# A state-space scan with its u and gate products in three passes on split operands, x split once for the scan and the heads

## The chip, the cores and the metric

The kernel is one program on one core of a Trainium2 chip. The metric is the device time of one execution in microseconds. TensorE is called PE in the rows, its weight loads PEld, VectorE DVE, ScalarE ACT, GpSimd POOL and the queue that issues the DMAs SP.

## What is computed

The program runs two transformer blocks one after the other, in fp32. The change lies in the mixer of the second block, which works on 512 tokens of width 1024. Of the reference it is this:

```
u = rmsnorm(x, mix_norm)
proj = u @ w_in
u_ssm, q, k, v, xq, g_ssm, g_attn, g_mem = jnp.split(proj, cuts, axis=-1)
y_ssm = jax.nn.gelu(s5_scan(u_ssm, ssm_a_re, ssm_a_im, ssm_log_dt, ssm_b_re, ssm_b_im,
                            ssm_c_re, ssm_c_im, ssm_d))
...
merged = (jax.nn.sigmoid(g_ssm) * br_ssm + jax.nn.sigmoid(g_attn) * br_attn
          + jax.nn.sigmoid(g_mem) * br_mem)
```

`s5_scan` is, for each of 32 groups of 16 channels, the recurrence x_t = A x_{t-1} + B u_t over 64 complex states, and y_t = Re(C x_t) + D u_t.

## The kernel before

Activations lie transposed, channels on the 128 partitions and the 512 tokens along the row, so x is 8 slices of 128 x 512 (KC is 8). A weight chunk is 128 x 1024: eight blocks of 128 x 128, which one product turns into one 128 x 512 output in PSUM. The accumulator `acc` is all of PSUM, eight banks of 128 x 512.

The mixer (`mixer_stage`) runs three stages one after the other, each a block with its own program for every engine: `scan_stage`, `heads_stage` and `out_stage`. Within a stage an engine runs its instructions in the order of the code, and semaphores are the only tie between engines; they start at 1. There is no scheduler.

**The scan stage** normalises x to `xn` (`m_xn`; L2082 on VectorE), and makes from it four chunks of u (L1944) and 24 chunks of gates (L1953), all with fp32 matmuls; one such matmul of 128 x 512 shows as two records in the trace. The four u chunks come as one load `s_w`; the gate chunks come through a ring of three buffers, `s_gw`. Then come small matrices: `b_wide` and `c_wide` are made by VectorE, transposed on TensorE (L1963, L1973) and copied by ScalarE to `s_b_t` and `s_c_t`.

The scan itself is a loop over SC = 16 steps of 128 complex states each:

- GpSimd makes the step's turns, the rotation by the angle at every token, with six operations of 128 x 512 (L1925 to L1928), in three buffers; it waits until step s-3 has used its buffer.
- TensorE makes the step's inputs (L1983, two fp32 matmuls, four records) two steps ahead.
- VectorE turns, scans and turns back (L2104 to L2126) and releases `scanned` with the last operation.
- TensorE then adds C times the state to y (L1998, four records).

The 24 gate products are spread over the steps: `at_step[s]` has two in an even step and one in an odd one. TensorE's order in step s is: the gates of s, the wait for `scanned` of s, y of s, inputs of s+2. ScalarE takes each gate from its bank through a sigmoid (L2018) and SP stores it.

**The heads stage** needs the same normed x for the query, key and value products. It does them in three passes on split operands: an operand is rounded to a shorter format on ScalarE (`hi`, type fp32r), the rest is what a subtraction of the rounded from the full value leaves (`lo`), and the product is hi x hi + hi x lo + lo x hi, three matmuls in place of one fp32 matmul. There x is rounded by ScalarE (L2517, L2520) and its rest taken by VectorE (L2648), and of each weight chunk ScalarE rounds (L2451) and GpSimd takes the rest (L2269), in a ring of four. Later the heads keep their queries and keys in the room of `xn`.

Of the kernel before, what the change touches and what calls it, by code (L numbers as in the profile page):

```python
# [69 lines left out]
        "c_in u_there gw0 gw1 gw2 sq_a sq_d summed rooted normed u_mm u_ready b_wid c_wid b_turned c_turned "  # L70
        "b_taken c_taken shape spun rotated bu_mm scanned y_mm y_pre gate_mm gated steady"),
    "d_": (
        "c_bd c_mem w0 w1 w2 w3 rounded split x_hi x_lo m_hi m_lo m_sq m_part m_mm m_root m_on proj_mm ev_a "
        "ev_d v_turn v_there scored logits expd weighed turned pt_there pv_mm took x_scored x_max x_exp "
        "x_weighed x_turned x_pt x_pv x_took"),
# [17 lines left out]
def build(nc, x_t, meta_t, mem_t, bias_onehot, dil_onehot, rel_bias, dil_table, gains, wi, wo, w_out,  # L93
# [3 lines left out]
    with top:  # L97
# [1590 lines left out]
        def mixer_stage(tables):  # L1688
            with ExitStack() as st:
# [3 lines left out]
                with ExitStack() as s1:  # L1693
                    xn = sb(s1, "m_xn", [P, KC, SEQ])
                    with ExitStack() as s2:
                        scan_stage(s2, xn, yg, tables)
                    with ExitStack() as s2:
                        heads_stage(s2, xn, at_, xa)
# [144 lines left out]
        def scan_stage(st, xn, yg, tables):  # L1843
# [7 lines left out]
            EARLY = 0  # L1851
            u = sb(st, "s_u_t", [P, 4, SEQ])
            b_t = sb(st, "s_b_t", [P, 2, 4, P])
            c_t = sb(st, "s_c_t", [P, 2, SC, P])
            d = sb(st, "s_dt", [P, 4])
            gw = sb(st, "s_gw", [P, 3, KC * P])
            gates = sb(st, "s_gates", [P, GATES_HELD, SEQ])
            w = sb(st, "s_w", [P, 4, KC * P])
# [11 lines left out]
            spare = sb(st, "s_spare", [P, SEQ])  # L1870
            rstd = spare
# [4 lines left out]
            (c_in, u_there, gw0, gw1, gw2, sq_a, sq_d, summed, rooted, normed, u_mm, u_ready, b_wid, c_wid, b_turned,  # L1876
             c_turned, b_taken, c_taken, shape, spun, rotated, bu_mm, scanned, y_mm, y_pre,
             gate_mm, gated, steady) = sems(st, "s_")
            gate_there = [gw0, gw1, gw2]
            at_step = [[n for n in range(EARLY, GATES) if (n - EARLY) * SC // (GATES - EARLY) == s] for s in range(SC)]  # L1880

            with nc.Block() as block:
                @block.sync
                def _(sp):
                    def store_gate(sp, n):
# [3 lines left out]
                    sp.dma_start(w[:, :, :], s_u.rearrange("c p n -> p c n")).then_inc(u_there, 16)  # L1889
# [4 lines left out]
                    for n in range(GATES):  # L1894
                        if n >= 3:
                            sp.wait_ge(gate_mm, 1 + n - 2)
                        sp.dma_start(gw[:, n % 3, :], gate_w[n]).then_inc(gate_there[n % 3], 16)
                        if n >= 3:
                            store_gate(sp, n - 3)
                    for n in range(GATES - 3, GATES):  # L1900
                        store_gate(sp, n)

                @block.gpsimd
                def _(pool):
# [6 lines left out]
                                       pattern=[[16, 8]], channel_multiplier=-1).then_inc(shape, 1)  # L1911
                    t = t_spare[:, :].rearrange("p (a b) -> p a b", a=COARSE)
                    for s in range(SC):
# [18 lines left out]
                        pool.drain()  # L1932
                    arm(pool, "d_")

                @block.tensor
                def _(pe):
                    pe.wait_ge(sq_a, 2)
                    pe.matmul(acc[:, 6, :], ones[:, :], nsq[:, 0, :], start=False, stop=True).then_inc(summed, 1)
                    pe.wait_ge(u_there, 17)
# [17 lines left out]
                    for n in range(EARLY):  # L1957
                        gate(n)
# [1106 lines left out]
```

## Time and profile before

| | us |
|---|---|
| median of three runs | 3737.55 (3736.84 to 3737.74) |
| the profiled execution | 3736.37 |
| its span, first to last instruction | 3734.7 |
| mean granted clock of TensorE | 0.976 |
| scan stage up to its first gate product, from 2691.5 | 48.4 |
| scan loop, 2739.90 to 2961.93 | 222.0 |
| end of the loop to the first matmul of the heads, 2972.55 | 10.6 |

In a timeline each row is one instruction, or several alike in a row (xN): start, length from the start of the first to the end of the last, engine, line, tiles written and read, and in brackets the idle time of that engine ahead of it with what ended it. Lengths of matmuls that follow each other overlap, so the time of one is read from start to start. In a windows row PEclk is TensorE's granted clock, in parts of 2.4 GHz.

### The profile page before, as it was taken

The numbers are of one execution on the slowest core, as the hardware profiler recorded it, in microseconds if no ns is written. First come the engines' busy times: TensorE is split into PE (matmuls) and PEld (weight loads), VectorE is DVE, ScalarE is ACT, GpSimd is POOL, SyncE is SP. The second block draws the span as 40 slices with busy tenths as digits, with TensorE's granted clock in tenths as the row PEclk, the third lists the DMA queues.
The fourth block names the chain that finished last, engine by engine and source line by source line (L and its number), as shares of the span: only waits on it lengthen the run. The fifth ranks groups of instructions, "written<-read, shape, count | busy, mean of one in ns | idle before, by whom it ended". The sixth has DMA issues, their size and how long they took to land. (4 is left out here: it accounts for less than half of the span.)

```text
span 3734.7 us, 50566 instructions
## 1 busy us (share of the span) xinstructions
PE 3566.8 (96%) x20104; PEld 2920.9 (78%) x20104; DVE 1741.1 (47%) x2492; ACT 1300.1 (35%) x1793; POOL 440.0 (12%) x465
## 2 busy tenths in 40 slices
PE   8999799799999999989999999999999899799998
PEld 7999777699999999755547888888744477678886
DVE  5442466544434443266625443443377533545433
ACT  4332266433323332134525432342110243324421
POOL 0000222100000000010006400000144233220000
PEclk9999899899999999989999999999999999999999
DMA  4322311022222222300013222222212421233222
GB/s 168 135 88 85 122 55 51 18 91 90 83 85 102 90 86 78 136 26 23 1 34 113 101 88 103 101 90 90 101 51 85 120 78 51 107 108 108 94 85 84
DMA packets 116172, 318.07 MB, mean 85 GB/s; under 512 B 13815, under 2 KB 56951, under 8 KB 100052
## 3 DMA queue, kind: packets, MB, share of 16 engines
q1 hardware_dynamic: 116052, 316.51, 25.0%
q8 instruction: 70, 1.15, 0.1%
q14 instruction: 50, 0.41, 0.0%
HBM read 307.98 MB, written 17.01 MB: 87 GB/s over the span
## 5 line engine op out<-in xcount | busy, mean ns | idle before, releaser
L332 PE MATMUL acc<-fb_xh,fb_wh 128*128 128x264 f32 x1408 | 287.8, 286 | 5.5 <-DVE fb_wl L489 5.5
L332 PE MATMUL acc<-fb_xl,fb_wh 128*128 128x264 f32 x1408 | 288.1, 286 | 0.0
L332 PE MATMUL acc<-fb_xh,fb_wl 128*128 128x264 f32 x1408 | 287.7, 286 | 0.0
L332 PE MATMUL acc<-fd_xh,fd_wh 128*128 128x512 f32 x704 | 275.6, 391 | 5.5 <-DVE fd_wl L489 5.5
L332 PE MATMUL acc<-fd_xl,fd_wh 128*128 128x512 f32 x704 | 274.6, 390 | 0.0
L332 PE MATMUL acc<-fd_xh,fd_wl 128*128 128x512 f32 x704 | 274.6, 390 | 0.0
L332 PEld LDWEIGHTS acc<-fb_xh,fb_wh 128*128 128x128 f32 x1408 | 220.1, 189 | 5.8 <-DVE fb_wl L489 5.7
L407 ACT ACTIVATE fb_wh<-fb_raw 128x2048 fp32r<-128x2048 f32 (+1 forms) x74 | 124.7, 1686 | 286.9 <-PE acc L391 173.8
L332 PEld LDWEIGHTS acc<-fb_xl,fb_wh 128*128 128x128 f32 x1408 | 219.3, 189 | 0.0
L332 PEld LDWEIGHTS acc<-fb_xh,fb_wl 128*128 128x128 f32 x1408 | 219.0, 189 | 0.0
L484 DVE TENSOR_TENSOR fb_wl<-fb_raw,fb_wh 128x2048 fp32r<-128x2048 f32 (+1 forms) x74 | 148.3, 2004 | 141.5 <-ACT fb_wh L407 140.6
L407 ACT ACTIVATE fd_wh<-fd_raw 128x2048 fp32r<-128x2048 f32 (+1 forms) x74 | 124.8, 1686 | 252.5 <-PE acc L391 159.3
L484 DVE TENSOR_TENSOR fd_wl<-fd_raw,fd_wh 128x2048 fp32r<-128x2048 f32 (+1 forms) x74 | 148.3, 2004 | 136.5 <-ACT fd_wh L407 135.6
L407 ACT ACT_TABLE_LOAD x60 | 77.0, 1283 | 301.3 <-PE acc L332 301.2
L1953 PE MATMUL acc<-m_xn,s_gw 128*128 128x512 f32 x384 | 169.0, 596 | 0.0
L332 PEld LDWEIGHTS acc<-fd_xh,fd_wh 128*128 128x128 f32 x704 | 132.7, 188 | 34.4 <-DVE fd_wl L489 6.3
L332 PEld LDWEIGHTS acc<-fd_xh,fd_wl 128*128 128x128 f32 x704 | 132.6, 188 | 27.9
L332 PEld LDWEIGHTS acc<-fd_xl,fd_wh 128*128 128x128 f32 x704 | 132.6, 188 | 27.7 <-issue 0.5
L689 POOL TENSOR_TENSOR a_wl<-a_raw,a_wh 128x1024 fp32r<-128x1024 f32 x32 | 76.0, 2376 | 661.0 <-ACT a_wh L885 661.0
L332 PE MATMUL acc<-fa_xh,fa_wh 128*128 128x264 f32 x704 | 144.3, 286 | 9.3 <-DVE fa_wl L489 9.3
L1953 PEld LDWEIGHTS acc<-m_xn,s_gw 128*128 128x128 f32 x384 | 71.7, 190 | 96.0 <-issue 96.0
L565 DVE SCALAR_TENSOR_TENSOR h<-acc,h 128x264 f32<-128x264 f32 (+1 forms) x72 | 35.1, 515 | 239.3 <-PE acc L391 239.3
(532 smaller groups left out, 8766.0 us busy)
## 6 DMA issues: line engine op xcount, KB each, us to landing
fb_raw<-wi_dram SPq DMA_DIRECT2D x42, 1024.0 KB, 4.8
fd_raw<-wi_dram SPq DMA_DIRECT2D x42, 1024.0 KB, 4.8
fb_raw<-wo_dram SPq DMA_DIRECT2D x32, 704.0 KB, 4.0
fd_raw<-wo_dram SPq DMA_DIRECT2D x32, 704.0 KB, 4.0
fa_raw<-wi_dram SPq DMA_DIRECT2D x20, 1024.0 KB, 4.8
ff_raw<-wi_dram SPq DMA_DIRECT2D x20, 1024.0 KB, 4.8
a_raw<-a_qkv_dram SPq DMA_DIRECT2D x24, 512.0 KB, 4.2
s_gw<-gate_w_dram SPq DMA_DIRECT2D x24, 512.0 KB, 3.8
```

What stands on the lines that cost most here:

```text
L332: last = pe.matmul(acc[:, up_base(p, b) + 2 * a + q, 0:w], x[:, k, a, :], part[:, k, t0:t0 + w], start=k == 0 and part is xh and x is wv, ...
L407: act.activation(wh[:, b, 0:n_], raw[:, b, 0:n_], ACT.Copy).then_inc(rounded, 1)
L484: dve.tensor_tensor(wl[:, b, 0:n_], raw[:, b, 0:n_], wh[:, b, 0:n_].bitcast(F32), ALU.subtract).then_inc(split, 1)
L565: last = dve.scalar_tensor_tensor(hv, acc[:, down_base(p) + 2 * (c % 2) + q, 0:w], 0.5, hv, ALU.mult, ALU.add)
L689: pool.tensor_tensor(wl[:, c % RING, :], raw[:, c % RING, :], wh[:, c % RING, :].bitcast(F32), ALU.subtract).then_inc(split, 1)
L1953: last = pe.matmul(acc[:, GATE_BANK[n % 2], :], gw[:, n % 3, k * P:(k + 1) * P], xn[:, k, :], start=k == 0, stop=k == KC - 1)
```

## The change

The scan stage makes its 28 products (four of u, 24 of gates) in three passes on split operands.

- `xn` of 8 slices is replaced by two buffers of one slice each, and by `xh` and `xl` (8 slices each), which are made in the scan stage and handed on to the heads. ScalarE rounds every slice; VectorE takes the rest of the even slices, GpSimd of the odd ones.
- The 28 weight chunks come through one ring of four. ScalarE rounds a chunk, GpSimd takes its rest, and TensorE waits for that (`split`). In the loop ScalarE rounds the chunk of gate n+2 ahead of the sigmoid of gate n, and GpSimd takes the rests of the gates n+2 behind the turns of the step that holds gate n.
- The heads stage loses its rounding and its splitting of x. A new tile `m_room` holds `s_c_t` in the scan and the queries and keys in the heads.

```diff
@@ scan_stage, gpsimd @@
+                    def rest_of_weights(j):
+                        pool.wait_ge(rounded, 1 + j + 1)
+                        pool.tensor_tensor(wl[:, j % RING, :], raw[:, j % RING, :],
+                                           wh[:, j % RING, :].bitcast(F32), ALU.subtract).then_inc(split, 1)
+
+                    rest_of_weights(0)
+                    for k in range(1, KC, 2):
+                        pool.wait_ge(x_hi, 1 + k + 1)
+                        pool.tensor_tensor(xl[:, k, :], xn[:, 1, :], xh[:, k, :].bitcast(F32),
+                                           ALU.subtract).then_inc(x_lo_p, 1)
+                        if k in (3, 5):
+                            rest_of_weights(k // 2)
+                    rest_of_weights(NU - 1)
...
                     for s in range(SC):
...
                         last.then_inc(spun, 1)
                         pool.drain()
+                        if s == 0:
+                            for j in range(NU, NU + AHEAD):
+                                rest_of_weights(j)
+                        for n in at_step[s]:
+                            if NU + n + AHEAD < CHUNKS:
+                                rest_of_weights(NU + n + AHEAD)
@@ scan_stage, tensor @@
-                    for c in range(4):
+                    def product(j, to):
+                        pe.wait_ge(split, 1 + j + 1)
                         for k in range(KC):
-                            if c == 0:
-                                pe.wait_ge(normed, 1 + k + 1)
-                            last = pe.matmul(acc[:, c, :], w[:, c, k * P:(k + 1) * P], xn[:, k, :],
-                                             start=k == 0, stop=k == KC - 1)
-                        last.then_inc(u_mm, 1)
+                            if j == 0:
+                                pe.wait_ge((x_lo_d, x_lo_p)[k % 2], 1 + k // 2 + 1)
+                            ks = slice(k * P, k * P + P)
+                            for x, part_ in ((wh, xh), (wh, xl), (wl, xh)):
+                                last = pe.matmul(to, x[:, j % RING, ks], part_[:, k, :],
+                                                 start=k == 0 and x is wh and part_ is xh,
+                                                 stop=k == KC - 1 and x is wl)
+                        return last
@@ scan_stage, scalar @@
+                    def round_weights(j):
+                        act.wait_ge(there[j % RING], 1 + 16 * (j // RING + 1))
+                        act.activation(wh[:, j % RING, :], raw[:, j % RING, :], ACT.Copy).then_inc(rounded, 1)
 
                     def gate(n):
+                        if NU + n + AHEAD < CHUNKS:
+                            if n >= AHEAD:
+                                act.wait_ge(gate_mm, 1 + n - AHEAD + 1)
+                            else:
+                                act.wait_ge(u_mm, 1 + n + NU - AHEAD + 1)
+                            round_weights(NU + n + AHEAD)
                         act.wait_ge(gate_mm, 1 + n + 1)
@@ scan_stage, vector @@
-                    for c in range(KC):
-                        dve.scalar_tensor_tensor(xn[:, c, :], h[:, c, META:], gain[:, 7, c:c + 1], rstd[:, :],
+                    for k in range(KC):
+                        if k >= 2:
+                            dve.wait_ge((x_lo_d, x_lo_p)[k % 2], 1 + k // 2)
+                        dve.scalar_tensor_tensor(xn[:, k % 2, :], h[:, k, META:], gain[:, 7, k:k + 1], rstd[:, :],
                                                  ALU.mult, ALU.mult).then_inc(normed, 1)
+                        if k % 2 == 0:
+                            dve.wait_ge(x_hi, 1 + k + 1)
+                            dve.tensor_tensor(xl[:, k, :], xn[:, 0, :], xh[:, k, :].bitcast(F32),
+                                              ALU.subtract).then_inc(x_lo_d, 1)
@@ heads_stage, scalar @@
-                    for k in range(4):
-                        act.activation(xh[:, k, :], xn[:, k, :], ACT.Copy).then_inc(x_hi, 1)
-                    round_weights(0)
-                    for k in range(4, KC):
-                        act.activation(xh[:, k, :], xn[:, k, :], ACT.Copy).then_inc(x_hi, 1)
-                    for j in range(1, RING):
+                    for j in range(RING):
                         round_weights(j)
@@ heads_stage, vector @@
-                    for k in range(KC):
-                        dve.wait_ge(x_hi, 1 + k + 1)
-                        dve.tensor_tensor(xl[:, k, :], xn[:, k, :], xh[:, k, :].bitcast(F32), ALU.subtract
-                                          ).then_inc(x_lo, 1)
```

What stands in a row on GpSimd in the scan stage before: the group mask `s_groups`, then the turns (`s_turns` from the tables `t_coarse` and `t_fine`), whose three rows come 32 times on end.

```order
L1905 MEMSET s_groups 128x8
L1907 AFFINE_SELECT s_groups<-s_groups 128x8
L1910 AFFINE_SELECT s_groups<-s_groups 128x8
L1925 TENSOR_TENSOR s_turns<-t_coarse,t_fine 128x512
L1926 TENSOR_TENSOR s_t_spare<-t_coarse,t_fine 128x512
L1928 TENSOR_TENSOR s_turns<-s_turns,s_t_spare 128x512
```

GpSimd in the changed kernel, from the end of step 0's turns to the rest behind step 1's (`s_wl` is the rest of a weight chunk):

```order
L1924 TENSOR_TENSOR s_wl<-s_raw,s_wh 128x1024 x4
L1948 TENSOR_TENSOR s_turns<-t_coarse,t_fine 128x512
L1949 TENSOR_TENSOR s_t_spare<-t_coarse,t_fine 128x512
L1951 TENSOR_TENSOR s_turns<-s_turns,s_t_spare 128x512
L1948 TENSOR_TENSOR s_turns<-t_coarse,t_fine 128x512
L1949 TENSOR_TENSOR s_t_spare<-t_coarse,t_fine 128x512
L1951 TENSOR_TENSOR s_turns<-s_turns,s_t_spare 128x512
L1924 TENSOR_TENSOR s_wl<-s_raw,s_wh 128x1024
```

Four rests (two of them for the first two gates) now stand between the turns of step 0 and those of step 1, one behind step 1, and from there two behind each even step and one behind each odd one.

ScalarE from the last u chunk to the gates, before:

```order
L2012 ACTIVATE s_u_t<-acc 128x512 x4
L2023 ACTIVATE s_b_t<-acc 128x1024
L2027 ACTIVATE s_c_t<-acc 128x512 x8
L2018 ACT_TABLE_LOAD
L2018 ACTIVATE s_gates<-acc 128x512 x24
```

And in the changed kernel (`s_wh` is a rounded weight chunk, `m_room` holds what `s_c_t` held):

```order
L2067 ACTIVATE s_b_t<-acc 128x1024
L2071 ACTIVATE m_room<-acc 128x512 x8
L2041 ACTIVATE s_wh<-s_raw 128x1024
L2053 ACT_TABLE_LOAD
L2053 ACTIVATE s_gates<-acc 128x512
L2041 ACTIVATE s_wh<-s_raw 128x1024
L2053 ACTIVATE s_gates<-acc 128x512
```

The rounding of a chunk now stands between every two sigmoids, and no table load beside the first.

VectorE from the reciprocal to the small matrices, in the changed kernel; before, all eight slices stood in one run:

```order
L2123 RECIPROCAL s_t_spare<-s_t_spare 128x512
L2128 SCALAR_TENSOR_TENSOR s_xn<-h,gain,s_t_spare 128x512
L2132 TENSOR_TENSOR m_xl<-s_xn,m_xh 128x512
L2128 SCALAR_TENSOR_TENSOR s_xn<-h,gain,s_t_spare 128x512 x2
L2132 TENSOR_TENSOR m_xl<-s_xn,m_xh 128x512
```

A rest of x (`m_xl`) now follows every other normed slice, and each waits for ScalarE's rounding of that slice.

## Rows read from the trace of the kernel before

**Rows 1.** The page: busy time and share of the span of each engine.
```profile
PE 3566.8 (96%) x20104; PEld 2920.9 (78%) x20104; DVE 1741.1 (47%) x2492; ACT 1300.1 (35%) x1793; POOL 440.0 (12%) x465
```

**Rows 2.** Timeline of PE, scan loop: start, us, line, tiles, count, wait.
```profile
2739.90 14.00 PE L1953 MATMUL acc<-m_xn,s_gw 128*128 128x512 f32 x32
2753.74 1.88 PE L1998 MATMUL acc<-s_work,s_c_t 128*128 128x512 f32 x4
2755.55 1.98 PE L1983 MATMUL acc<-s_u_t,s_b_t 32*128 32x512 f32 x4
2757.46 7.13 PE L1953 MATMUL acc<-m_xn,s_gw 128*128 128x512 f32 x16
...
2768.15 14.00 PE L1953 MATMUL acc<-m_xn,s_gw 128*128 128x512 f32 x32
```

**Rows 3.** Busy time in a window: us, engines (x records), PEclk, DMA.
```profile
2740.00:2961.00 221.00, 221.00 (x503) 92.95 (x504) 163.13 (x226) 14.46 (x25) 86.20 (x78) 1.00 0.26 78
```

**Rows 4.** Timeline of DVE, first scan steps (columns as in rows 2).
```profile
2739.31 0.69 DVE L2104 TENSOR_TENSOR s_work<-acc,s_turns 128x512 f32<-128x512 f32 x1 [15.10 <-issue]
...
2749.18 0.68 DVE L2126 TENSOR_TENSOR s_work<-acc,s_work 128x512 f32<-128x512 f32 x1
2750.02 0.69 DVE L2104 TENSOR_TENSOR s_work<-acc,s_turns 128x512 f32<-128x512 f32 x1 [0.16 <-issue]
```

**Rows 5.** Timeline of POOL, the turns of one step and the next.
```profile
2748.56 1.04 POOL L1925 TENSOR_TENSOR s_turns<-t_coarse,t_fine 128x512 f32<-128x512 f32 x1 [32.41 <-DVE acc L2121]
...
2754.36 1.26 POOL L1928 TENSOR_TENSOR s_turns<-s_turns,s_t_spare 128x512 f32<-128x512 f32 x1
2759.28 1.05 POOL L1925 TENSOR_TENSOR s_turns<-t_coarse,t_fine 128x512 f32<-128x512 f32 x1 [3.65 <-DVE acc L2121]
```

**Rows 6.** Timelines of ACT, then DVE: a gate, then takes in the heads.
```profile
2753.94 0.60 ACT L2018 ACTIVATE s_gates<-acc 128x512 f32<-128x512 f32 x1 [6.27 <-PE acc L1953]
...
2996.62 0.60 ACT L2466 ACTIVATE d_vt<-acc 128x512 f32<-128x512 f32 x1 [3.76 <-PE acc L2281]
2997.12 1.05 ACT L2451 ACTIVATE d_wh<-d_raw 128x1024 fp32r<-128x1024 f32 x1
...
2991.18 0.69 DVE L2595 COPY m_xn<-acc 64x512 f32<-64x512 f32 x1 [4.74 <-PE acc L2281]
```

**Rows 7.** Timeline of POOL, the first rest of weights in the heads.
```profile
2970.14 2.35 POOL L2269 TENSOR_TENSOR d_wl<-d_raw,d_wh 128x1024 fp32r<-128x1024 f32 x1 [55.02 <-ACT d_wh L2451]
```

**Rows 8.** Timeline of PE, scan's start; then PEclk (after POOL) in windows.
```profile
2699.48 6.34 PE L1944 MATMUL acc<-m_xn,s_w 128*128 128x512 f32 x10 [6.13 <-DMA s_w<-s_u_dram]
...
2709.27 21.73 PE L1944 MATMUL acc<-m_xn,s_w 128*128 128x512 f32 x50 [0.55 <-DVE m_xn L2082]
...
2696.00:2699.40 3.40, 0.00 (x0) 0.00 (x0) 3.31 (x3) 0.00 (x0) 3.26 (x3) 0.50 1.02 399
...
2702.80:2706.00 3.20, 3.02 (x7) 0.87 (x5) 3.20 (x3) 0.00 (x0) 3.06 (x3) 0.99 0.28 110
```

**Rows 9.** Timeline of DVE: normed slices; rests of x without, with POOL.
```profile
2697.64 11.57 DVE L2082 SCALAR_TENSOR_TENSOR m_xn<-h,gain,s_spare 128x512 f32<-128x512 f32 x8
...
2965.28 2.50 DVE L2648 TENSOR_TENSOR d_xl<-m_xn,d_xh 128x512 fp32r<-128x512 f32 x4 [2.56 <-ACT d_xh L2517]
...
2970.62 2.43 DVE L2648 TENSOR_TENSOR d_xl<-m_xn,d_xh 128x512 fp32r<-128x512 f32 x1 [2.84 <-ACT d_xh L2520]
```

**Rows 10.** Timelines at the heads' start: ACT, then PE.
```profile
2969.01 1.06 ACT L2451 ACTIVATE d_wh<-d_raw 128x1024 fp32r<-128x1024 f32 x1 [2.20 <-DMA d_raw<-d_qkv_dram]
...
2972.55 0.79 PE L2281 MATMUL acc<-d_xh,d_wh 128*128 128x512 f32 x1 [10.62 <-POOL d_wl L2269]
```

**Rows 11.** Timelines: last c_wide on DVE, first transpose, loop's end on PE.
```profile
2720.95 3.26 DVE L2092 TENSOR_SCALAR s_work<-s_c_in,s_groups 128x512 f32<-128x512 f32 x8
...
2730.83 1.04 PE L1963 MATMUL acc<-ident,s_b_wide 128*128 128x128 f32 x8
...
2960.05 1.88 PE L1998 MATMUL acc<-s_work,s_c_t 128*128 128x512 f32 x4
```

More of the change, by code:

```diff
@@ L1875, in scan_stage @@
             xs = work[:, 6:10, :].rearrange("p (j r) t -> p j r t", j=2)
[L1876 to L1880, printed above, removed]
+            (c_in, w0, w1, w2, w3, rounded, split, sq_a, summed, rooted, normed, x_hi, x_lo_d, x_lo_p, u_mm, u_ready,
+             b_wid, c_wid, b_turned, c_turned, b_taken, c_taken, shape, spun, rotated, bu_mm, scanned, y_mm, y_pre,
+             gate_mm, gated) = sems(st, "s_")
+            there = [w0, w1, w2, w3]
+            at_step = [[n for n in range(GATES) if n * SC // GATES == s] for s in range(SC)]
             with nc.Block() as block:
@@ L1893, in _ @@
                     sp.dma_start(d[:, :], s_d).then_inc(c_in, 16)
[L1894 to L1901, printed above, removed]
+                    for j in range(1, RING):
+                        weights(j)
+                    STORED_AFTER = NU + 6
+                    for j in range(RING, CHUNKS):
+                        sp.wait_ge(split, 1 + j - RING + 1)
+                        weights(j)
+                        if j >= STORED_AFTER:
+                            store_gate(j - STORED_AFTER)
+                    for n in range(CHUNKS - STORED_AFTER, GATES):
+                        store_gate(n)
                 @block.gpsimd
@@ L2018, in gate @@
                         act.activation(gates[:, n % GATES_HELD, :], acc[:, GATE_BANK[n % 2], :], ACT.Sigmoid).then_inc(gated, 1)
-                    for n in range(EARLY):
-                        gate(n)
+                    round_weights(0)
+                    for k in range(KC):
+                        act.wait_ge(normed, 1 + k + 1)
+                        act.activation(xh[:, k, :], xn[:, k % 2, :], ACT.Copy).then_inc(x_hi, 1)
+                        if k in (2, 4, 6):
+                            round_weights(k // 2)
+                    for c in range(NU):
+                        act.wait_ge(u_mm, 1 + c + 1)
+                        if c < AHEAD:
+                            round_weights(c + RING)
+                        act.activation(u[:, c, :], acc[:, c, :], ACT.Copy).then_inc(u_ready, 1)
                     act.wait_ge(b_turned, 2)
@@ L2028, in _ @@
                                        acc[:, 2 + n % 2, :], ACT.Copy).then_inc(c_taken, 1)
-                    for n in range(EARLY, GATES):
+                    for n in range(GATES):
                         gate(n)
@@ L2298, in unit @@
                         else:
-                            last = product(at_chunk[(kind, n)], acc[:, b, :], xh, xl, first=j == 0)
+                            last = product(at_chunk[(kind, n)], acc[:, b, :], xh, xl)
                         last.then_inc(proj_mm, 1)
```

70 lines of the change are left out of this document (33 added, 37 removed).

## The prediction

> **What bounds the kernel now.** I read the page first: TensorE (PE) is busy 96% of a span of 3734.7 us [rows 1], so an edit pays only if it shortens TensorE's work and opens no new wait. The change is in the scan, so I then read TensorE's timeline there. The scan loop has 16 steps. In an even step TensorE runs two gate products (24 products over 16 steps: two, one, two, one), in an odd step one; then the output matmuls y of the step, then the input matmuls of the step two later. The reader is to see in [rows 2] that no row has a wait: 32 gate matmuls from 2739.90, y from 2753.74, inputs from 2755.55, one product from 2757.46, and the next even step at 2768.15. Two steps take 28.25 us: three products at 6.92 (13.84 for two) and twice 3.72 for y and inputs. [Rows 3] say the same of the loop: 221.00 of 221.00 us busy, clock 1.00, VectorE 163 us, GpSimd 86 us. A step on VectorE takes 10.55 us to its last operation and 10.71 to the next step (2739.31, 2749.18 + 0.68, 2750.02) [rows 4]; two need 21.4 of the 28.25. The turned angles of a step cost GpSimd 2748.56 to 2754.36 + 1.26, thus 7.06 us, then it waits for VectorE [rows 5]: it is ahead. The loop ends at 2960.05 + 1.88 = 2961.93 [rows 11], 222.0 us after 2739.90.
>
> **The products.** A product of eight fp32 matmuls (16 records) becomes 24 matmuls on rounded operands. The heads run that form already: from take to take 4.74 + 0.69 = 5.43 us for 24 of them at full clock [rows 6], 0.226 each. So a product falls from 6.92 to 5.43, and 28 products would give back 28 x 1.49 = 41.7 us if TensorE had no wait. That is what a sum over TensorE alone says; the rest of this part is on why it does not get it.
>
> **The chain that the change closes.** GpSimd now takes the rest of each weight chunk, once ScalarE has rounded it, and in its program this stands behind the turns of a step and ahead of the turns of the next. After step s it takes the rests of gate n+2 for every gate n of step s. ScalarE rounds the chunk of gate n+2 only after the sigmoid of gate n-1, which waits for product n-1. For an even step the second of its two gates needs the first product of the same step. So GpSimd stands in its wait until TensorE has done that product, and the turns of the following odd step are queued behind it; VectorE waits for these turns, TensorE's y of the odd step waits for VectorE, and the next even step's products stand behind that y. One round of this chain takes two steps. Its legs: first product 5.43; to the sigmoid 0.20 (2753.74 to 2753.94) and from one ScalarE operation to the end of the rounding 0.50 + 1.05 [rows 2, 6]; rest of weights 0.07 + 2.35 [rows 7]; turns with the gap ahead of them 0.14 + 7.06 [rows 5]; VectorE 0.10 + 10.55 [rows 4]; y and inputs 0.10 + 3.72 [rows 2]. The sum is 31.3 us, against 28.25 now and against 23.75 for TensorE's own work (3 x 5.43 + 2 x 3.72). The saving is gone and 3 us more. Ring of four, rounding two chunks ahead: neither cuts the chain, since what is late is the turns, not the weights.
>
> **The clock in it.** In the odd step TensorE is done with its product 10.87 + 3.72 + 5.43 = 20.0 us into the round and waits until 31.3 - 3.8 = 27.5: an idle time of 7.5 us. After 6.13 us of idle time the clock stood at 0.50 from 2696.0 and was back at 0.99 in the window from 2702.8, and the ten matmuls that ran there took 6.34 instead of 10 x 0.4325 + 0.16 = 4.49 [rows 8]: 1.85 us lost. The same matmuls of y and inputs come first behind the new idle time and lie on the chain. Bounds for this term are 0 (the clock holds) and 3.7 (low twice as long); I take 1.8, by the nearest row, since 7.5 is more than 6.13. A round is then 33.1 us.
>
> **The loop.** The chain closes from step 0 to step 12, seven rounds of 33.1 = 231.7; behind step 14 no chunk is left to wait for, and the last two steps are 10.87 + 1.81 + 5.43 + 1.88 = 20.0 from TensorE's own work, with VectorE done in time (its step 15 ends 15.8 into them). 251.7 against 222.0: **+29.7 us**.
>
> **The front.** The slices of x are now rounded and split ahead of the first product: eight normed slices and four rests on VectorE, four rests of x and four rests of weights on GpSimd. Both engines have two operands in SBUF here. Beside GpSimd the eight normed slices took 11.57 us, 1.45 each; four rests of x took 2.50 without GpSimd (0.62 each), and one took 2.43 beside a rest of weights that ran until 2972.49, 0.56 us ahead of its end [rows 7, 9]. So they take turns by whole instructions: 12 x 0.62 + 4 x 2.35 + 4 x 1.26 = 21.9 us, of which 19.6 stand ahead of the last rest of x (the last rest of weights follows it), and some 1.7 of ScalarE's roundings that nothing covers. The normed slices start at 2697.64 [rows 9]; I let the first rest of weights start 1 us ahead of them, as its chunk is by then loaded and rounded. That ends near 2717.9. TensorE has then 3 matmuls of the first product and 72 more, 17.0 us, and 1.8 for a clock that is low after short bursts: 2736.7. Now the first transpose stands at 2730.83 [rows 11]. **+5.9 us**; the 6 us that the four u products give back are in it. Bounds: with no turn-taking the last rest of x would be at 2714.0 and the clock full, +0.3; with each of the twelve VectorE operations at 2.43, +14.8. VectorE's small matrices need 15.0 us behind its last slice (2709.21 to 2724.21) [rows 9, 11]; from 2715.9 they end at 2730.9 and stay hidden behind u. If the front took TensorE's cover down to there, they would be the next in line.
>
> The Trainium skill says in "SBUF — State Buffer" (SBUF: two separate sides) that VectorE with two SBUF inputs and GpSimd hold one pair of ports as a lock for the whole instruction, and that the loser stops. By that rule the term is near +5.9; by sharing without a lock it would be nearer +0.3. The 2.43 us row agrees with it. "GPSIMD Engine Reference" (4.1 Engine selection) sends two-input work on a tile to VectorE, which speaks against this change.
>
> **The heads.** They no longer round and split x. Their first matmul stood at 2972.55 behind a rest of weights and a rounding that waited for the DMA of the weights (2.20 us of idle time ahead of 2969.01) [rows 7, 10]. All that stays, so what goes was hidden. I take -0.5 for the slower first product, with ends 0 and -1.7. Gate stores, loads and evictions of gates fall into TensorE's longer loop and cost nothing; if the loop got short they would still be one DMA per 8 us.
>
> **The sum.** 29.7 + 5.9 - 0.5 = 35.1 us. The profiled execution took 3736.4 us (1.7 around its span) and the median of three is 3737.6: 3736.4 + 35.1 + 1.2 = **3772.5 us**.
>
> **Rivals.** (1) The chain closes, but the clock holds or its low time falls mostly into idle time: seven times 1.8 and the 1.8 of the front go, 3758. For it: low times begin some us after the idle time; against: 6.13 us sufficed [rows 8]. (2) The other side: the turns of the odd step are out before VectorE needs them, and TensorE stays the bound. It decides at the point where the rest ahead of these turns can start without the step's first product. The place would be the same wait. Then a round is 23.75 (the first has 0.6 of waiting), the loop 24.4 + 6 x 23.75 + 20.0 = 186.9, -35.1; with the front and the heads -29.7: 3708. For it: GpSimd has 86 of 221 us of work and 28 x 2.35 more is still under the loop. Against: share is not order, and the order ahead of the turns is fixed. (3) Worse: the front at its upper bound (+8.9), or the clock low twice as long in each round (+12.6): about 3783. (4) The gain of a front that costs nothing and half-open chains cancel: within 0.2%, 7.5 us, which is also about what a measurement tells from no change.
>
> **How the numbers follow.** Main case 0.66, by itself 3764 to 3780 (front +0.3 to +10). Rival 1 0.15, rival 3 0.09, rival 2 0.08, rival 4 0.02. The range takes in rival 1 and rival 3 up to their bounds, 3755 to 3786, and leaves out rivals 2 and 4. Faster 0.08, same 0.02, slower 0.90.
>
> **What would show it.** In the changed kernel's trace TensorE's y of odd steps waits 7 to 8 us, seven times, for VectorE; VectorE waits for the turns; GpSimd's rests wait for ScalarE, and the next even step starts 33 us after the last. The clock has a low stretch in each round. The first transpose stands near 2736.7. If y never waits and products follow at 5.43, the chain is wrong and rival 2 right; if rounds take 31.3 at clock 1.00, rival 1. A product far from 5.43, or another price for the turns, would break the sum.

## The result and the profile after

The changed kernel took 3795.73 us (median of four, 3792.31 to 3806.39), the kernel before on the same chip 3737.62. The ratio is 1.0163, with a 95% interval from 1.0151 to 1.0175: slower by 56 to 65 us. The prediction said slower, 3772.5 us, with a range up to 3786. The sign held, the size did not: 23.2 us are missing from the sum, and the time lies above the range.

The page of the kernel after, with the row that answers to [rows 1]: TensorE's share fell from 96% to 94% though its busy time rose a little, and GpSimd has 69 us more.

```profile
PE 3569.5 (94%) x20328; PEld 2979.3 (79%) x20328; DVE 1742.8 (46%) x2488; ACT 1327.8 (35%) x1821; POOL 509.0 (13%) x497
```

**The front.** From the scan's first matmul (2692.22 before, 2693.61 after) the first transpose stood 38.61 us behind it before and stands 45.19 behind it now: +6.6, where +5.9 was predicted. The timelines of VectorE and then GpSimd, at two of the slices (columns as in [rows 2]):

```profile
2713.54 2.85 DVE L2128 SCALAR_TENSOR_TENSOR s_xn<-h,gain,s_t_spare 128x512 f32<-128x512 f32 x1
...
2718.44 2.34 DVE L2096 TENSOR_TENSOR s_v<-s_a_in 128x16 f32<-128x16 f32 x1
...
2713.03 2.82 POOL L1924 TENSOR_TENSOR s_wl<-s_raw,s_wh 128x1024 fp32r<-128x1024 f32 x1
2717.14 1.26 POOL L1930 TENSOR_TENSOR m_xl<-s_xn,m_xh 128x512 fp32r<-128x512 f32 x1 [1.29 <-ACT m_xh L2058]
```

A normed slice (L2128), 0.75 us by itself, takes 2.85 beside a rest of weights of 2.82: it ends at 2716.39, 0.54 us behind the end of that rest (2715.85), so it waited for the whole of it. The last rest of x (L1930) ends at 2718.4 (predicted 2717.9). A VectorE operation on only 128 x 16 (L2096, 0.16 us by itself) takes 2.34 beside another rest, and both end within 0.03 us of each other.

**The loop.** TensorE's waits from 2690 to 3060, by what ended them (us in total, times, longest):

```profile
PE acc L2027 <- DVE s_work L2176: 48.0, 7, 7.2
PE acc L2327 <- POOL d_wl L2317: 10.6, 1, 10.6
```

Seven waits of y for VectorE, 48.0 us, 6.9 each: the wait that the prediction named, as often as it said (7 to 8 us was its size). The chain behind the first of them, on ScalarE, GpSimd, VectorE and TensorE in turn:

```profile
2753.78 0.60 ACT L2053 ACTIVATE s_gates<-acc 128x512 f32<-128x512 f32 x1 [5.63 <-PE acc L1976]
2754.27 1.05 ACT L2041 ACTIVATE s_wh<-s_raw 128x1024 fp32r<-128x1024 f32 x1
...
2755.40 2.40 POOL L1924 TENSOR_TENSOR s_wl<-s_raw,s_wh 128x1024 fp32r<-128x1024 f32 x1 [6.10 <-ACT s_wh L2041]
...
2763.57 1.29 POOL L1951 TENSOR_TENSOR s_turns<-s_turns,s_t_spare 128x512 f32<-128x512 f32 x1
...
2764.96 0.69 DVE L2154 TENSOR_TENSOR s_work<-acc,s_turns 128x512 f32<-128x512 f32 x1 [7.12 <-POOL s_turns L1951]
2765.02 2.42 POOL L1924 TENSOR_TENSOR s_wl<-s_raw,s_wh 128x1024 fp32r<-128x1024 f32 x1 [0.16 <-issue]
2765.57 0.68 DVE L2155 TENSOR_TENSOR s_work<-acc,s_turns 128x512 f32<-128x512 f32 x1
...
2774.84 0.68 DVE L2176 TENSOR_TENSOR s_work<-acc,s_work 128x512 f32<-128x512 f32 x1
...
2775.57 3.74 PE L2027 MATMUL acc<-s_work,m_room 128*128 128x512 f32 x4 [6.82 <-DVE s_work L2176]
2779.24 1.98 PE L2012 MATMUL acc<-s_u_t,s_b_t 32*128 32x512 f32 x4
2781.15 0.50 PE L1976 MATMUL acc<-m_xh,s_wh 128*128 128x512 f32 x1
```

Read it downwards. The sigmoid of the step's first product (2753.78), then the rounding of the next chunk, then GpSimd's rest of it, which had waited 6.10 us for the rounding; only behind that rest come the turns of the odd step (the last at 2763.57), for which VectorE had waited 7.12; VectorE is done at 2774.84 + 0.68 and y starts at 2775.57, after 6.82 us of idle time. The two rows from 2765.02 show that GpSimd does not slow VectorE here as it does in the front: with one operand in PSUM (`acc`) VectorE's operation takes 0.68 us beside a rest of weights.

What is new is the price behind the wait. Here y took 3.74 us where 1.88 is its time at full clock. The same place in the fourth round, on TensorE, and last a window over the stretch in which the clock was low:

```profile
2879.53 3.78 PE L2027 MATMUL acc<-s_work,m_room 128*128 128x512 f32 x4 [6.79 <-DVE s_work L2176]
2883.24 3.77 PE L2012 MATMUL acc<-s_u_t,s_b_t 32*128 32x512 f32 x4
2886.95 0.79 PE L1976 MATMUL acc<-m_xh,s_wh 128*128 128x512 f32 x1
...
2891.38 0.58 PE L1976 MATMUL acc<-m_xl,s_wh 128*128 128x512 f32 x1
2891.80 0.40 PE L1976 MATMUL acc<-m_xh,s_wl 128*128 128x512 f32 x1
...
2874.60:2891.60 17.00, 12.07 (x19) 6.02 (x20) 14.74 (x21) 0.00 (x0) 5.87 (x5) 0.50 0.12 43
```

Now y takes 3.78, the inputs (L2012) 3.77 instead of 1.98, and the product's first eleven matmuls 0.43 us from one to the next instead of 0.23. In the last line, whose columns are those of [rows 3], the number behind GpSimd's is the granted clock: 0.50 for 17.0 us, thus 1.2 GHz of 2.4. It fell in the idle time, which ended at 2879.53, and came back only inside the product. In the first two rounds the low stretch was 6.8 us long. In the first it ran from 2772.3 to 2779.1 and was over before the inputs, in the second it reached 0.7 us into them; in the third it was 13.7 us long, from the fourth on 17.1.

The seven rounds, from the first product of an even step to that of the next (2747.87 to 2999.47), took 33.28, 33.65, 35.11, 37.04, 37.30, 37.40 and 37.82 us, together 251.6; predicted were seven of 33.1, 231.7. The rest of the loop, to its last y at 3020.31 + 1.88, took 22.7 (predicted 20.0). The heads' first matmul now waits 10.6 us for its rest of weights, as before [rows 10].

### The profile page after: what moved, and what is told of

Read it like the earlier page. It is cut to its first block and busy times, and to the rows that moved or that the text cites. A ratio compares the mean times of both kernels' runs of the same rounds, so it can differ in the third digit from the quotient of the medians.

```text
span 3794.0 us, 51098 instructions
## 1 busy us (share of the span) xinstructions
PE 3569.5 (94%) x20328; PEld 2979.3 (79%) x20328; DVE 1742.8 (46%) x2488; ACT 1327.8 (35%) x1821; POOL 509.0 (13%) x497
## 5 line engine op out<-in xcount | busy, mean ns | idle before, releaser
L1436 POOL TENSOR_TENSOR b_work<-b_work 128x512 f32<-128x512 f32 x16 | 20.8, 1301 | 950.4 <-ACT b_work L1564 950.4
L332 PE MATMUL acc<-fa_xl,fa_wh 128*128 128x264 f32 x704 | 144.5, 287 | 0.0
```

Of the source, the lines that this page charges most:

```text
L332: last = pe.matmul(acc[:, up_base(p, b) + 2 * a + q, 0:w], x[:, k, a, :], part[:, k, t0:t0 + w], start=k == 0 and part is xh and x is wv, ...
L1436: pool.tensor_tensor(sq_sum[:, hd % 2, :], sq[:, hd % 2, 0, :], sq[:, hd % 2, 1, :], ALU.add).then_inc(added_sq, 1)
```

## The experiments

All are edits of the changed kernel. Three theories stood: the closed chain costs the saving; the low clock is what the forecast sized too small; and the two engines that share x and the weights in the front cost the rest. The kernel before took 3737.2 us beside the first four, and 3736.0 beside the last three, which ran on another chip; where kernels of the two groups are compared, the distance of each from the kernel before on its own chip counts.

**Turns ahead of the rests.** Nothing else is moved: GpSimd takes the rests of a step's gates behind the turns of the next step (`rests_behind` holds the lines that are taken out below).

```diff
@@ scan_stage, gpsimd @@
                     for s in range(SC):
...
                         last.then_inc(spun, 1)
                         pool.drain()
-                        if s == 0:
-                            for j in range(NU, NU + AHEAD):
-                                rest_of_weights(j)
-                        for n in at_step[s]:
-                            if NU + n + AHEAD < CHUNKS:
-                                rest_of_weights(NU + n + AHEAD)
+                        if s:
+                            rests_behind(s - 1)
```

> Only GpSimd's order in the scan loop changes: the turns of step s+1 go ahead of the rests of weights that stood behind the turns of step s. Theory A (the turns queued behind a rest that waits for the same step's first product close a chain through GpSimd, VectorE and TensorE): the waits of y for VectorE vanish but for under 1 us in step 1, the clock stays at 1.00, and the loop falls from 274 us to TensorE's own work, 24 x 5.60 + 16 x 1.81 + 14 x 1.91 + 0.6 = 191, so about 3712 us in all, 0.7% below the kernel before. Theory B (three passes on split operands keep GpSimd and VectorE on the same memory, so steps are slow whatever the order): waits of several us stay and the time stays above 3770.

Measured: 3718.51 us (3715.81 to 3721.05), ratio 0.9951 [0.9934, 0.9967]. The order of two kinds of work on GpSimd is worth 77 us, and undoing it alone makes the change a gain. The loop, from the first inputs to the end of the last y, fell from 277.0 to 194.3 us (before the change: 224.7), and no y waits. Why it is 6 us above the expectation shows in TensorE's waits and timeline ahead of the loop:

```profile
PE acc L2006 <- DVE s_work L2146: 4.6, 1, 4.6
...
2744.55 6.69 PE L2006 MATMUL acc<-ident,s_work 128*128 128x128 f32 x32 [4.60 <-DVE s_work L2146]
```

The turns of step 1 now stand ahead of the loop, beside VectorE's small matrices. These came 4.60 us late, and the transposes behind that idle time ran at low clock: 6.69 us for 32, where 8 took 1.04 in [rows 11]. The first inputs stand 57.3 us behind the scan's first matmul, 51.6 in the changed kernel.

**The clock kept, the chain left.** TensorE gets seven throwaway fp32 matmuls ahead of y in odd steps, where it would be idle.

```diff
@@ scan_stage, tensor @@
                             gate(n)
+                        if s % 2 and s < SC - 1:
+                            n = at_step[s][-1]
+                            pe.wait_ge(gated, 1 + n)
+                            for _ in range(7):
+                                pe.matmul(acc[:, GATE_BANK[(n + 1) % 2], :], ident[:, :], u[:, 0, :],
+                                          start=True, stop=True)
                         pe.wait_ge(scanned, 1 + s + 1)
```

> The changed kernel with its order, and in the seven odd steps that wait seven throwaway fp32 matmuls (6.05 us at full clock) into a free bank ahead of the wait for VectorE, so that TensorE has no idle time of 7 us. They are extra work. Theory A (a round is 31.4 us of chain plus 5.2 us of matmuls run at the low clock): a round falls from up to 37.5 to 31.4 to 31.8 us, the clock stays at 1.00, and the total falls by 30 to 35 us to about 3763, although TensorE does more. Theory B (the excess over 31.4 is a wait or contention that has nothing to do with the clock): no gain, or 6 us more a round, 3795 to 3840.

Measured: 3759.96 us (3759.26 to 3762.04), ratio 1.0064 [1.0047, 1.0080]. More work, 35.8 us less time. The waits of y are down to 1.2 us and less, and the clock of the whole stretch is full. TensorE's timeline at the place of the rows above, and one window over five rounds of this kernel and then of the changed one:

```profile
2766.05 6.17 PE L2027 MATMUL acc<-s_u_t,ident 128*128 128x512 f32 x14
2773.04 1.99 PE L2033 MATMUL acc<-s_work,m_room 128*128 128x512 f32 x4 [0.82 <-DVE s_work L2182]
2774.96 1.98 PE L2012 MATMUL acc<-s_u_t,s_b_t 32*128 32x512 f32 x4
2776.86 0.50 PE L1976 MATMUL acc<-m_xh,s_wh 128*128 128x512 f32 x1
...
2760.00:2935.00 175.00, 170.18 (x560) 102.86 (x560) 116.51 (x163) 24.68 (x32) 115.42 (x85) 1.00 0.21 73
```

```profile
2760.00:2935.00 175.00, 140.96 (x427) 87.06 (x426) 102.33 (x142) 22.52 (x29) 98.32 (x73) 0.82 0.19 66
```

The fillers (14 records, 6.17 us) take the place of the idle time; y starts 2.5 us sooner on the page only because the whole stage stands 2.5 us earlier. From there y takes 1.99 and the inputs 1.98, at a granted clock of 1.00 over the five rounds, against 0.82. The seven rounds take 31.52, 31.52, 31.51, 31.50, 31.50, 31.50 and 31.86 us, 220.9 in all. So the chain by itself is 31.5 us a round (the prediction's legs gave 31.3), and what the low clock cost the changed kernel's rounds is 251.6 - 220.9 = 30.7 us, 4.4 each, where the prediction took 1.8.

**The chain opened on ScalarE.** ScalarE rounds each chunk one gate earlier, so that the rest ahead of an odd step's turns needs no product of the same step; GpSimd's order is left as the change has it.

```diff
@@ scan_stage, scalar @@
                     def gate(n):
-                        if NU + n + AHEAD < CHUNKS:
-                            if n >= AHEAD:
-                                act.wait_ge(gate_mm, 1 + n - AHEAD + 1)
-                            else:
-                                act.wait_ge(u_mm, 1 + n + NU - AHEAD + 1)
-                            round_weights(NU + n + AHEAD)
+                        if n == 0:
+                            act.wait_ge(u_mm, 1 + NU)
+                            round_weights(NU + AHEAD)
+                            round_weights(NU + AHEAD + 1)
+                        elif NU + n + AHEAD + 1 < CHUNKS:
+                            act.wait_ge(gate_mm, 1 + n)
+                            round_weights(NU + n + AHEAD + 1)
                         act.wait_ge(gate_mm, 1 + n + 1)
```

> Only ScalarE's order changes: the chunk of gate n+3 is rounded ahead of the sigmoid of gate n (it was n+2), so the rest that stands ahead of an odd step's turns no longer needs a product of the same step. GpSimd's order is that of the changed kernel. Theory A: the chain is cut at another link, so this gives the same as moving the turns, 3710 to 3716 us. Theory B (GpSimd's place in the order matters by itself, because it has too much to do): 3750 or more.

Measured: 3713.35 us (3712.99 to 3713.49), ratio 0.9937 [0.9921, 0.9954]; inside the expectation. GpSimd's wait ahead of the odd step's turns is short now, and TensorE is busy 174.3 of the 175 us in the window that held 141.0 in the changed kernel:

```profile
2791.09 2.40 POOL L1924 TENSOR_TENSOR s_wl<-s_raw,s_wh 128x1024 fp32r<-128x1024 f32 x1 [0.16 <-issue]
2796.47 2.34 POOL L1924 TENSOR_TENSOR s_wl<-s_raw,s_wh 128x1024 fp32r<-128x1024 f32 x1 [2.98 <-ACT s_wh L2041]
2798.78 1.05 POOL L1948 TENSOR_TENSOR s_turns<-t_coarse,t_fine 128x512 f32<-128x512 f32 x1
...
2760.00:2935.00 175.00, 174.27 (x627) 115.17 (x626) 151.40 (x211) 31.10 (x41) 140.23 (x104) 1.00 0.24 82
...
PE acc L2027 <- DVE s_work L2177: 0.7, 1, 0.7
```

The first two rows are the two rests behind step 4, the third starts the turns of step 5. In the changed kernel the second of two such rests, here behind step 2, waited 11.72 us instead of 2.98:

```profile
2788.68 2.39 POOL L1924 TENSOR_TENSOR s_wl<-s_raw,s_wh 128x1024 fp32r<-128x1024 f32 x1 [11.72 <-ACT s_wh L2041]
```

What is left of the wait (2.8 to 3.0 us a round) no longer reaches TensorE: in the whole loop one y waits, for 0.7 us. From the second round on a round takes 24.4 us: three products of 5.60 and twice 3.72, which is 24.2, and 0.2 because the first matmul of a product behind other matmuls takes 0.34 in place of 0.23 (2747.87 to 2748.21 in the changed kernel). The loop took 195.2 us. So the same tie, cut at two different places, gives the same loop within 1 us; it was the tie, not the count of GpSimd's instructions, that closed the chain.

**The rests of x on VectorE alone.** On top of the turns put first, VectorE takes all eight rests of x, one slice behind, and GpSimd takes its three rests of the u weights once six of these are done.

```diff
@@ scan_stage, gpsimd @@
-                    for k in range(1, KC, 2):
-                        pool.wait_ge(x_hi, 1 + k + 1)
-                        pool.tensor_tensor(xl[:, k, :], xn[:, 1, :], xh[:, k, :].bitcast(F32),
-                                           ALU.subtract).then_inc(x_lo_p, 1)
-                        if k in (3, 5):
-                            rest_of_weights(k // 2)
-                    rest_of_weights(NU - 1)
+                    pool.wait_ge(x_lo_d, 1 + KC - 2)
+                    for j in range(1, NU):
+                        rest_of_weights(j)
+                    pool.wait_ge(x_lo_d, 1 + KC)
```

> As the kernel with the turns first, and in the front all eight rests of x on VectorE, one slice behind the normed slices, with the three later rests of weights on GpSimd only when six rests of x are done. Theory A (VectorE with two operands in SBUF and GpSimd take turns by whole instructions, and GpSimd's rests of weights of 2.4 to 2.8 us stand between the slices): the last slice is split near 2710 instead of 2718.4, the u products are done some 8 to 10 us sooner, total 3702 to 3705. Theory B (the front is bound by the hand-over from engine to engine per slice): within 2 us of the kernel with the turns first.

Measured: 3714.45 us (3713.15 to 3714.53), ratio 0.9939 [0.9922, 0.9956]. A miss by 10 us: only 4 us under the kernel with the turns first, which is neither of the two forecasts. The first six slices went as hoped, the end did not. VectorE's timeline, then GpSimd's:

```profile
2706.95 0.75 DVE L2130 SCALAR_TENSOR_TENSOR s_xn<-h,gain,s_t_spare 128x512 f32<-128x512 f32 x1
2707.62 0.68 DVE L2134 TENSOR_TENSOR m_xl<-s_xn,m_xh 128x512 fp32r<-128x512 f32 x1
2708.34 2.95 DVE L2130 SCALAR_TENSOR_TENSOR s_xn<-h,gain,s_t_spare 128x512 f32<-128x512 f32 x1
2711.22 5.59 DVE L2134 TENSOR_TENSOR m_xl<-s_xn,m_xh 128x512 fp32r<-128x512 f32 x2
...
2708.39 7.87 POOL L1924 TENSOR_TENSOR s_wl<-s_raw,s_wh 128x1024 fp32r<-128x1024 f32 x3 [8.96 <-DVE m_xl L2134]
```

A slice and its rest take 0.75 + 0.68 while GpSimd stands still (2706.95, 2707.62). Then GpSimd starts three rests of weights in a row, and the last three VectorE operations take 2.95 and 5.59 beside them: 8.5 us instead of 2.1. The overlap was small in count and still ate the saving.

**The same with GpSimd held until all eight are done.** With ScalarE's early rounding in place of the turns put first. The lines are those that differ, in GpSimd's front, from the kernel just above.

```diff
@@ scan_stage, gpsimd @@
-                    pool.wait_ge(x_lo_d, 1 + KC - 2)
+                    pool.wait_ge(x_lo_d, 1 + KC)
                     for j in range(1, NU):
                         rest_of_weights(j)
-                    pool.wait_ge(x_lo_d, 1 + KC)
```

> The kernel with the early rounding, and in the front all eight rests of x on VectorE while GpSimd keeps still: its rests of weights 1 to 3 come only when the last rest of x is done (the run with x on VectorE let them in after the sixth, and three of them then stood ahead of VectorE's last three operations, 8.5 us for what takes 2.1). Theory A (turn-taking by whole instructions sets the front): eight slices take 8 x 1.39 us, the last near 2709.8, the first rest of weights behind it near 2712.2, three more products 16.8 us and 1.8 for the low clock, so the first transpose stands some 6 us sooner than with the early rounding alone, 3707 us in all. Theory B (only the place of the wait moves: VectorE's small matrices are late instead): within 2 us of 3713.

Measured: 3711.30 us (3710.71 to 3712.25), ratio 0.9934 [0.9917, 0.9950]. The last rest of x ends at 2711.2, and the first transpose stands 39.1 us behind the scan's first matmul (before 38.6, after 45.2): what the front lost up to there is gone. Yet the time is 24.7 us under the kernel before, and early rounding alone had 23.9: less than 1 us of gain. The 3707 expected was missed, and what the second theory named (the small matrices late instead) is what happened. TensorE's waits and VectorE's timeline say where it went:

```profile
PE acc L1998 <- DVE s_work L2140: 2.6, 1, 2.6
PE acc L1988 <- DVE s_b_wide L2117: 2.2, 1, 2.2
...
2710.47 0.69 DVE L2130 TENSOR_TENSOR m_xl<-s_xn,m_xh 128x512 fp32r<-128x512 f32 x1 [0.17 <-ACT m_xh L2055]
...
2713.64 2.38 DVE L2093 TENSOR_TENSOR s_v<-s_a_in 128x16 f32<-128x16 f32 x1
...
2728.60 2.46 DVE L2111 TENSOR_TENSOR s_bbar<-s_b_in,s_v 128x256 f32<-128x256 f32 x1
...
2733.23 3.26 DVE L2140 TENSOR_SCALAR s_work<-s_c_in,s_groups 128x512 f32<-128x512 f32 x8
```

From the last rest of x to the start of `c_wide` (L2140) VectorE needs 22.1 us (2711.2 to 2733.23) for its small matrices; in [rows 9, 11] it was 11.7 (2709.21 to 2720.95). Operations on 128 x 16 take 2.38 and on 128 x 256 2.46, each about as long as a rest of weights, three of which take 7.11 us and then two 4.93. TensorE now waits for them, 2.6 and 2.2 us, and its first inputs stand 49.5 us behind the scan's first matmul, where they stood at 45.0 before and at 51.6 in the changed kernel. This is what the prediction said of the front: with TensorE's cover taken down, the small matrices are next in line.

**The turns behind the small matrices too.** One line more:

```diff
@@ scan_stage, gpsimd @@
                     for j in range(1, NU):
                         rest_of_weights(j)
+                    pool.wait_ge(c_wid, 2)
```

> As the one before, and GpSimd starts the turns only when VectorE's small matrices (b_wide, c_wide) are made. Theory A: these matrices then take the 13 to 15 us that they need without GpSimd beside them and end some us before the u products do; no wait of TensorE for them is left, and turns of step 0 (7 us) still end before the first step. Same time as the one before if that had no such wait, up to 4 us less if it had: 3703 to 3707. Theory B: step 0's turns are late and the loop starts 3 to 7 us later, 3710 or more.

Measured: 3706.89 us (3700.91 to 3711.50), ratio 0.9925 [0.9909, 0.9942]; inside the expectation. The best of all kernels here: 29 us under the kernel before on the same chip, where the changed kernel was 58 above it on its own. VectorE's `c_wide` operations, then GpSimd's rests of weights and the turns behind them:

```profile
2720.96 3.26 DVE L2141 TENSOR_SCALAR s_work<-s_c_in,s_groups 128x512 f32<-128x512 f32 x8
...
2707.97 7.10 POOL L1924 TENSOR_TENSOR s_wl<-s_raw,s_wh 128x1024 fp32r<-128x1024 f32 x3 [11.21 <-DVE m_xl L2131]
2724.30 1.05 POOL L1945 TENSOR_TENSOR s_turns<-t_coarse,t_fine 128x512 f32<-128x512 f32 x1 [9.23 <-DVE s_work L2141]
```

The turns now start at 2724.30, when `c_wide` is done; only three rests of weights still stand beside the small matrices. From the last rest of x (2707.9) it is 13.1 us to `c_wide`, and the waits for `s_work` and `s_b_wide` ahead of the loop are gone. The first inputs stand 43.1 us behind the scan's first matmul; 49.5 without this line, 45.0 before the change. Of these 6.4 us the medians show 4.4, and this kernel's runs spread over 10.6 us, so the size of the step is the profile's; that it is a gain rests on the rows, and on three of its four runs, which lie under all of the other's. The later turns have a price of their own: y of step 1 waits 1.9 us, 1.1 without this line.

**The inputs on 128 rows.** Back to the changed kernel with its chain closed. The inputs' matmuls use all 128 rows instead of the 32 of their groups. The scan's inputs are then not the reference's; nothing is taken away, and every wait stays.

```diff
@@ scan_stage, tensor @@
-    b_t[js, r, c, :], u[js, c, :]
+    b_t[:, r, c, :], u[:, c, :]
```

> The changed kernel, but the input matmuls of the scan read all 128 rows of b_t and u in place of the step's 32, so the scan gets other inputs than the reference's; number, columns and order of the matmuls stay. In the changed kernel's trace the first two rounds take 33.3 and 33.7 us and the later ones 37 and more: there the low clock lasts through y, the inputs and the next product. Theory A (it stays low since y and the small 32-row inputs come first behind the idle time): the clock is back within y or the inputs in every round, rounds stay near 33 to 34 us, and the total falls by 15 to 20 us to about 3778. Theory B (it depends only on when the matmuls start again, whatever they are): rounds of 37 us and 3792 to 3800 as before.

Measured: 3778.85 us (3775.42 to 3781.95), ratio 1.0117 [1.0100, 1.0133]. As expected, 16.9 us less than the changed kernel; by the distance to the kernel before on the same chip it is 15.3, and the seven rounds together took 236.1 us instead of 251.6. The place of its fourth round that answers to 2879.53 above, the low stretch there, and the window over five rounds:

```profile
2875.27 3.78 PE L2027 MATMUL acc<-s_work,m_room 128*128 128x512 f32 x4 [7.20 <-DVE s_work L2176]
2878.84 2.95 PE L2012 MATMUL acc<-s_u_t,s_b_t 128*128 128x512 f32 x4
2881.22 0.80 PE L1976 MATMUL acc<-m_xh,s_wh 128*128 128x512 f32 x1
2881.86 0.40 PE L1976 MATMUL acc<-m_xl,s_wh 128*128 128x512 f32 x1
2882.09 0.39 PE L1976 MATMUL acc<-m_xh,s_wl 128*128 128x512 f32 x1
...
2870.50:2880.50 10.00, 5.23 (x6) 2.18 (x7) 9.38 (x14) 0.00 (x0) 5.71 (x5) 0.51 0.17 63
2760.00:2935.00 175.00, 139.00 (x468) 91.99 (x467) 104.55 (x146) 24.00 (x31) 108.71 (x80) 0.87 0.20 71
```

The idle time is the same or longer (7.20 us), y is as slow (3.78), but the clock is back from the product's second matmul on (0.23 apart), where the changed kernel needed eleven of them. The low stretch is 10.2 us long instead of 17.1 (it begins 0.2 us into the first window), the clock over five rounds 0.87 instead of 0.82, and a late round takes 34.1 us instead of 37.4. A part of that is the matmuls' own: at full clock y, the inputs and the product's first matmul take 3.67 us (2759.12 to 2762.79) against 4.06 in the changed kernel (2759.18 to 2763.24), 0.4 a round. The other 2.9 are the clock's. In this kernel, then, the clock comes back later behind 32-row inputs than behind 128-row ones; why, the run does not tell.

One rival has to be looked at: a shorter round also moves the idle time against the moment at which the clock falls. In the changed kernel it fell 3.6, 4.4 and 4.9 us into the idle time of rounds one to three and stayed low for 6.8, 6.8 and 13.7 us; from the fourth on it fell after 2.0 to 2.5 us and stayed low for 17.1. With 128-row inputs it fell after 3.4 and 5.0 us and stayed low for 6.8, and from the third round on after 2.3 to 3.0 us and stayed low for 10.2. So the moment of the fall and the length of the stretch do change together, but where the clock fell at a like moment (near 4.9, and near 2.4) the stretch was shorter with 128 rows (6.8 against 13.7, 10.2 against 17.1).

## Why the prediction was wrong in size

**The chain: right.** Order, place, count and size held. The waits are where it put them, seven of 6.9 us (7.5 by its sum), and with the clock kept a round takes 31.5 us against 31.3 of the legs. Rival 2, that the turns come out in time, fell: it is what the kernels with the tie cut show, with a round of 24.4 us where it reckoned 23.75.

**The clock in it: the step that failed.** The term was 1.8 us a round with bounds 0 and 3.7, from ten matmuls behind 6.13 us of idle time [rows 8]. It measured 30.7 us over seven rounds, 4.4 each, and in the late rounds 5.9. What was wrong was to carry over the price of the nearest row: there the low stretch was 6.8 us, of which 3.5 were still idle time, and 128-row matmuls ran in the rest. Here y and then 32-row inputs run first, and the low stretch grows from 6.8 us in the first two rounds to 17.1 from the fourth on and reaches into the product. In the fourth round 12.2 of its 17.1 us lie behind the start of y. Even the upper bound, low twice as long, was under it. That is 18.1 of the 23.2 missing us, and the low clock behind the last round another 2.2. Rival 3 named the mechanism, but its 3783 rested on the same price, too low.

**The product: 5.43, measured 5.60.** I took the interval between two takes of early heads' products [rows 6], 0.226 us per matmul. Here they follow at 0.233 (19 starts from 2754.75 to 2758.95, 18 intervals). On the chain it is one product a round: 7 x 0.17 = 1.2 us, and 0.5 in the last two steps; in the front another 0.5. Why some run at 0.227 and most at 0.233 stays open; nothing here was run for it.

**The front: right in mechanism, in part by luck in size.** +6.6 against +5.9. Two errors inside it cancel in part: counted from the scan's first matmul, the last rest of x ended 0.9 us sooner than in the sum, and TensorE's work behind it took 20.35 us (2718.45 to 2738.80) where the sum had 18.8. Of that the low clock, until 2724.5, cost 2.8 instead of 1.8, and the slower product 0.5. The lower bound's 2714.0 for the last rest of x comes in the prediction without its terms. The small matrices, next in line by the prediction once TensorE's cover is gone, were so in the fifth kernel. The turn-taking by whole instructions is in the rows, 2.85 beside 2.82, and the experiments show its inverse: with GpSimd still a slice and its rest take 1.4 us, and the first transpose comes 6.1 us sooner. The rule of the Trainium skill in "SBUF — State Buffer" (SBUF: two separate sides), that VectorE and GpSimd hold the shared ports for the whole instruction, agrees with these rows; the sum by sharing without that lock, +0.3, does not. The Trainium skill's "GPSIMD Engine Reference" (4.1 Engine selection), which sends two-input work on a tile to VectorE, held for the rests of x: one takes 1.26 us on GpSimd (L1930) and 0.69 on VectorE with GpSimd still.

**The heads, the rest.** The idle time ahead of the heads' first matmul is 10.59 us against 10.62. The heads' first product did not get the 0.5 us faster that the sum had: it took 8.29 us instead of 7.55, with the clock low there for 13.7 us instead of 10.2. Behind it the kernel is 1.7 us shorter, at places that I did not look for. The scan's first matmul stands 1.4 us later on the page than before; it lies between 2690.55 and 2694.89 in all nine kernels, which do the same ahead of it, so it looks like scatter between programs rather than the change.

**The account.** Rounds 18.1 + 1.2 and 0.6 of small gaps; the last two steps 2.7; the front 0.7, the heads 0.5, the scan's start 1.4, and what follows the heads' first matmul -0.9; the 1.2 that I added for the median against the profiled run was not there (3795.70 profiled, 3795.73 median), -1.2. Together 23.1 of 23.2.

## What to carry to other kernels

Before a faster product is booked as a gain, follow what the engine that now feeds it has queued behind its new wait: here one rest of weights ahead of one step's turns cost 77 us, and moving it behind them, or its rounding one gate earlier, turned +58 us into -19 and -24. An idle time on the chain costs itself and then the clock: price what runs at half speed behind it from the very matmuls that stand there, and let the upper bound be all of them at half speed. In a stretch where VectorE is on the path, keep GpSimd still rather than share the work with it, small operations included; in the scan loop, where VectorE's operations have one operand in PSUM, they kept their 0.7 us beside GpSimd.

## What was not expected of the hardware

- With the same idle time of 6.8 us ahead of y, and the same matmuls behind it, the clock was low for 6.8 us in the first two rounds and for 17.1 from the fourth on; with inputs on 128 rows, and 7.2 us of idle time, for 10.2. The longer stretches began sooner in the idle time, after 2.0 to 2.5 us instead of 3.6 and 4.4. Why is open.
- Seven throwaway matmuls a round in the idle time made the changed kernel 35.8 us faster, at a clock of 1.00 instead of 0.82 over five rounds.
- A VectorE operation of 0.16 us on 128 x 16 elements takes up to 2.38 beside a GpSimd operation of 2.37. The small matrices went from 11.7 to 22.1 us that way. Operations with a single tensor operand are not spared: in the kernel with the turns first the one on 128 x 256 ahead of `c_wide` took 2.33 us, and 0.30 before.
